# Order of the first recurrent mixer's output projection: one unit of the second half ahead of the first half's rest

## The reference

```
hmod = rms_norm(x, g_pre) * (1 + scale) + shift
y    = rms_norm(fn(hmod), g_post)
x    = x + weight * gate * y
```

```
hs = hs * rsqrt(mean(hs*hs) + EPS)                  # per head
hs = hs.reshape(B, S, 1024) * norm_w * sigmoid(o)
y  = hs @ ml_w_out                                  # 1024 x 1024
```

## Time and profile before

| | us |
|---|---|
| median of three runs | 1425.66 |
| lowest and highest run | 1424.58, 1426.38 |
| span of the profiled execution | 1421.9 |
| runs' median less that span | 3.8 |
| TensorE busy in the span | 1394.5 |
| VectorE busy | 1024.9 |
| ScalarE busy | 719.7 |
| mean granted clock, share of full | 0.998 |

### The profile page before, as it was taken

How to read it: one execution, slowest core, us unless ns; L and a number is a source line. 1 busy time by engine, 2 the same in 40 slices (tenths; PEclk the granted TensorE clock), 3 DMA queues, 4 the chain that set the end, 5 groups by cost and what they waited for, 6 DMA issues and landing times.

```text
span 1421.9 us, 18024 instructions
## 1 busy us (share of the span) xinstructions
PE 1394.5 (98%) x7310; PEld 1185.4 (83%) x7310; DVE 1024.9 (72%) x1296; ACT 719.7 (51%) x931; POOL 90.4 (6%) x118
## 2 busy tenths in 40 slices
PE   9999999998999999999999999999999999999997
PEld 8788888977888878888789978788888889998886
DVE  5887677987987668777767976678745654664865
ACT  5543356456444455343565676554334644555433
POOL 1000001001000010000000352100000100000000
PEclk9999999999999999999999999999999999999999
DMA  9898865855988848888535522478755454445542
GB/s 385 339 351 303 319 247 198 320 193 201 391 308 298 325 162 324 318 311 332 200 135 186 209 74 89 178 299 336 283 206 207 178 204 167 148 170 186 199 149 111
DMA packets 50498, 339.07 MB, mean 238 GB/s; under 512 B 6720, under 2 KB 8432, under 8 KB 10352
## 3 DMA queue, kind: packets, MB, share of 16 engines
q1 hardware_dynamic: 50416, 337.92, 63.8%
HBM read 336.81 MB, written 2.66 MB: 239 GB/s over the span
## 4 chain that ended last, share of the span: by engine, by line
PE 78%; DVE 12%; ACT 4%; DMA 2%; issue 2%; POOL 1%; SPq 0%; ACTq 0%; DVEq 0%; POOLq 0%
PE ps L1045 76%; DVE wlo L1704 4%; DMA raw<-units 2%; DVE hf L2126 2%; DVE M L1714 1%; ACT whi L558 1%; PE ps L1263 1%; PE ps L1154 1%; ACT hf L639 0%; POOL base L474 0%; POOL ssx L475 0%; DVE xboth L1779 0%; DVE wlo L1709 0%; PE ps L1528 0%; DVE xboth L2061 0%
## 5 line engine op out<-in xcount | busy, mean ns | idle before, releaser
L1045 PE MATMUL ps<-whi,xboth 128*128 128x512 f32 x2864 | 912.2, 393 | 6.5 <-DVE wlo L1709 1.7
L1045 PEld LDWEIGHTS ps<-whi,xboth 128*128 128x128 f32 x2864 | 538.3, 188 | 125.4 <-issue 4.7
L1704 DVE TENSOR_TENSOR wlo<-raw,whi 128x2048 fp32r<-128x2048 f32 x212 | 486.2, 2298 | 178.5 <-ACT whi L558 178.0
L1045 PE MATMUL ps<-wlo,xboth 128*128 128x512 f32 x1432 | 558.5, 390 | 0.0
L558 ACT ACTIVATE whi<-raw 128x2048 fp32r<-128x2048 f32 x218 | 416.9, 1915 | 170.8 <-DMA raw<-units 170.7
L1045 PEld LDWEIGHTS ps<-wlo,xboth 128*128 128x128 f32 x1432 | 269.5, 188 | 52.6
L1045 PE MATMUL ps<-xboth,whi 128*128 128x256 f32 (+1 forms) x1152 | 254.6, 310 | 0.1
L1045 PEld LDWEIGHTS ps<-xboth,whi 128*128 128x128 f32 x1152 | 187.9, 190 | 12.4 <-ACT hf L829 0.3
L1045 PE MATMUL ps<-xboth,wlo 128*128 128x256 f32 x704 | 198.1, 281 | 0.0
L1714 DVE SCALAR_TENSOR_TENSOR M<-M 128x1024 f32<-128x1024 f32 x160 | 189.3, 1220 | 0.1
L1045 PEld LDWEIGHTS ps<-xboth,wlo 128*128 128x128 f32 x704 | 133.9, 190 | 0.0
(11 more groups left out here) (242 smaller groups left out, 881.2 us busy)
## 6 DMA issues: line engine op xcount, KB each, us to landing
raw<-units SPq DMA_DIRECT2D x218, 1024.0 KB, 4.9
M<-ada_units SPq DMA_DIRECT2D x82, 1024.0 KB, 7.1
M<-units SPq DMA_DIRECT2D x10, 1024.0 KB, 5.3
gp<-gate_rows SPq DMA_DIRECT2D x7, 512.0 KB, 6.1
bias_copies<-bias_by_distance SPq DMA_DIRECT2D x1, 1536.0 KB, 9.6
M<-cvec SPq DMA_DIRECT2D x2, 512.0 KB, 4.4
x<-x_in SPq DMA_DIRECT2D x1, 1024.0 KB, 6.0
ada_a<-ada_units SPq DMA_DIRECT2D x1, 1024.0 KB, 20.0
```

The costliest lines, as they stand in the source:

```text
L1045: return pe.matmul(out, lhsT, rhs, start=start, stop=stop, skip_group_check=True)
L1704: dve.tensor_tensor(rest(u), landed(u), rounded(u).bitcast(F32), ALU.subtract).then_inc(w_lo, 1)
```

## The change

The loop over halves and units becomes a written list: (0,0), (1,0), (0,1), (0,2), (0,3), (1,1), (1,2), (1,3). `turn_am(1, (0, 1))`, the turns of the last head pair for both halves, stands between (0,0) and (1,0). The waits for `ml_lo`, the turn of the next stage's rows in the middle of (1,3), the `w_used` of half 1 and `y_done[0]` at the end of (0,3) are kept. No other engine's list is touched.

```diff
-                    for t in range(T):
-                        for u in range(4):
-                            if t == 0 and u == 2:
-                                turn_am(1, (1,))
-                            pe.wait_ge(S["ml_lo"], 2 * (u // 2) + t + 1)
-                            middle = None
-                            if (t, u) == (0, 1):
-                                middle = lambda: turn_am(1, (0,))
-                            if (t, u) == (1, 3):
-                                middle = lambda: turn_x(n + 1, 0)
-                            r = down(u0 + 12 + u, 2 * u, t, start=(u == 0), stop=(u == 3), middle=middle)
-                            if t:
-                                r.then_inc(w_used, 1)
-                        if t == 0:
+                    for t, u in ((0, 0), (1, 0), (0, 1), (0, 2), (0, 3), (1, 1), (1, 2), (1, 3)):
+                        if (t, u) == (1, 0):
+                            turn_am(1, (0, 1))
+                        pe.wait_ge(S["ml_lo"], 2 * (u // 2) + t + 1)
+                        r = down(u0 + 12 + u, 2 * u, t, start=(u == 0), stop=(u == 3),
+                                 middle=(lambda: turn_x(n + 1, 0)) if (t, u) == (1, 3) else None)
+                        if t:
+                            r.then_inc(w_used, 1)
+                        elif u == 3:
                             r.then_inc(y_done[0], 1)
```

## The result

The changed kernel takes 1429.29 us (median of 8 runs, 1427.93 to 1433.01), the kernel before 1425.53 us (8 runs beside it, 1423.03 to 1427.76). The ratio is 1.0025, 95% interval 1.0013 to 1.0036: slower by 3.6 us (1.9 to 5.1). The ratio is not the quotient of the two medians, so the two can differ by a few ten-thousandths. The forecast was 1428.9. The profiled execution took 1428.32 us with a span of 1426.5.

A forecast was written before the change was run, and what follows sets the result against it. TensorE, busy 98% of the span, was taken as the bound, so only its idle time counts. 0 us of work plus 3.27 us of waits on 1425.66 gave 1428.9 us; range 1426.6 to 1431.1.

The forecast's parts named there:

- The waits at the turns: First recurrent mixer's output projection: TensorE waits of 2.22 + 0.37 us for DVE's gating replace 1.61 us of waits.
- The first half's result: End of (0,3) in the projection: last product starts 3.56 us later, 2.72 of it from (1,0) moved ahead.
- The boundary: Boundary to the next feed-forward stage: DVE's fixed order passes on 3.27 us to TensorE's last release, at 341.87.
- what falls away on DVE: In the boundary, DVE's 0.29 us wait for ACT at 325.06 disappears, as ACT's work is only 2.0 us later.
- The wait at the turns of the rows: In the boundary, TensorE reaches the normed rows' turns before DVE's rows are ready and waits 1.0 us.
- The clock: Behind the turns, a possible fall to 1.2 GHz costing 1.7 us of lost work, left out of the sum.
- signs of being wrong: L1801 shifted but not TensorE's restart; granted clock under 1 between 306 and 312 us; first turns earlier than 305.
- the bound worked out from the earlier trace: From a clock fall behind a thin stretch at 820.0 in another stage: 1.7 us of lost work.
- The rival that I gave 0.17: The clock falls behind the new gap at the turns: +4.97 us in all, 1430.6 us; chance 0.17.
- the clock's case: The total if the clock falls behind the gap at the turns: +4.97 us, 1430.6 us; chance 0.17.
- Slower or the same: Whole kernel: 0.61 slower, 0.37 same, 0.02 faster, with about 0.2%, or 2.9 us, needed to tell a change.
- Queues: Load queue: unit 12's slot comes free at 309.4 instead of 316.7 us, the load lands earlier, worth nothing.

The follow-up runs named there:

- e3: Kernel before with only (1,0) moved ahead of (0,3), turns and their waits as before: 1427.18 us against 1425.06, ratio 1.0022.
- e5: Kernel before with only the turns of both halves moved between (0,0) and (0,1), old order of products: 1426.97 us against 1425.19, ratio 1.0016.
- r2: Changed kernel run again unchanged to see whether the clock falls: 1429.59 us (one run) against 1425.05 for the kernel before.
- r3: Changed kernel run again unchanged to see whether the clock falls: 1426.22 us (one run) against 1425.05 for the kernel before.
- r1: Changed kernel run again unchanged to see whether the clock falls: 1428.55 us against 1425.05 for the kernel before, ratio 1.0018.
- r4: Kernel before with DVE's last-pair gating ahead of unit 14's lower part and the first half's turns half a unit earlier, repeated: 1422.78 us against 1425.05, ratio 0.9984.
- e8: Changed kernel with DVE's last-pair gating ahead of unit 14's lower part and its last sums before its wait: 1425.64 us against 1425.19 (kernel before), ratio 1.0007.
- e1: Changed kernel with nine small products of ones between (0,0) and the turns, keeping TensorE busy: 1427.74 us against 1425.06 (kernel before), ratio 1.0021.

## Why the prediction was right

**The waits at the turns.** Predicted 2.22 + 0.37 us, with the turns at 305.39 and 306.17. Found at 305.39 and 306.17, less the offset.

**The first half's result.** Predicted 3.56 us late; 3.57, 3.58 and 3.52 in the profiles whose clock held. Apart: 2.72 for (1,0) (e3: 2.71) and 0.84 for the waits (e5: 0.82). The sum of the parts is the whole.

**The boundary.** Predicted to pass on 3.27; it passed on 3.16 to 3.21. The term that was a little off is what falls away on DVE, which I had as 0.29 us. From L1770 to the third of the lower parts (L1779, now L1774) DVE takes 4.97 us now and took 5.50, so 0.53 us of waiting for ACT fell away; POOL took some of it back (below). The wait at the turns of the rows was predicted at 1.0 us and is 0.98.

**The clock.** I left it out of the sum, because the gap of 2.22 us was nearer to the waits that had left the clock alone. It should have been a term with a chance of its own; two of four profiles say about a half, roughly. A granted clock under 1 between 306 and 312 us is among the prediction's own signs of being wrong, and the first profile shows it, at 0.72; r2 and r3 do not. The measured price, 1.6 us, is that of the bound worked out from the earlier trace rows, 1.7. The rival that I gave 0.17 was seen in two of four profiles of the changed kernel: in these four an execution is either about +3.2 or +4.8 at the last release. At even chances the mean is +4.0, an estimate from these figures. The Trainium skill ("TensorE: Matmul & The Clock Gate", Part 1) has idleness as what brings the half rate back; the trace agrees, and shows that one and the same gap does it in some executions only.

**What is luck in the number.** The forecast missed the median by 0.4 us. The interval of the measured loss is 1.9 to 5.1 us, so it holds the forecast's 3.3, the 4.0 with the clock in it and also the clock's case, 4.8. In r1 the two medians are 3.5 us apart, and the ratio gives 2.6. The mechanism is confirmed by the places in the profiles; the closeness of the total is partly luck.

**Slower or the same.** With 3.3 expected against 2.9 to be told, I gave 0.61 to slower by over 0.2%. The ratio is 0.25%, and r1 gave 0.18% with the interval 0.07 to 0.30: a loss is certain, its side of 0.2% is not.

**Queues.** That the earlier slot is worth nothing was not tried alone. ACT's wait for that load is gone and nothing behind it came earlier.

## What to carry to other kernels

A wait that is removed from the bound engine can be worth nothing if the removal delays what the next stage's serial chain starts from; ask which result leaves the stage first, and put no unit ahead of it. Here the cure for most of the waiting was on the engine that was waited for: its urgent operation belonged ahead of one that nobody needed yet. And a wait that is gathered in one place can cost more than the same waiting spread out: behind the gap of 2.2 us the clock fell in two of the changed kernel's four profiles.

## What the runs showed of the hardware

**The clock's fall is a matter of the single execution.** Beside the gap here, the second recurrent mixer has two places where the clock falls in some profiles, about 824 and 872 us. Two stretches of it in r4, then in e8:

```profile
820.00:840.00 20.00, 18.25 (x122) 15.10 (x122) 13.10 (x11) 16.02 (x33) 11.12 (x8) 1.00 0.15 53
860.00:880.00 20.00, 18.57 (x119) 16.25 (x119) 15.82 (x24) 13.79 (x31) 6.98 (x6) 1.00 0.03 5
```

```profile
820.00:840.00 20.00, 18.66 (x104) 15.15 (x102) 8.80 (x8) 13.55 (x29) 7.67 (x6) 0.83 0.15 53
860.00:880.00 20.00, 17.57 (x111) 15.92 (x111) 13.30 (x19) 13.99 (x37) 6.83 (x4) 0.83 0.08 35
```

The stage between the turns of the normed rows at its two ends takes 210.68 to 210.76 us in the four profiles without a fall there, 212.31 to 212.61 in the seven with one, 213.68 and 213.91 in two more, and 216.45 in e8, in which each of the two stretches has a mean of 0.83. No edit touches this stage. By the granted clock each fall costs 1.7 us of work, those in e8 twice that, as 0.83 over 20 us says; the stage is 1.6 to 1.9 us longer with one, 3.0 to 3.2 with two and 5.7 in e8. Why e8's last longer is not known. This is much of the spread of 2 to 8 us between runs of one kernel: of the 35 runs of the kernel before in the session of e1, the seven with a mean granted clock of 0.999 took 1421.8 to 1423.8 us, the three with 0.994 or 0.995 took 1428.8 to 1429.3. It is the reason why edits of 1 us had to be read in the profile, from a row near them, and not in the time. Up to 2.4 us more vary between TensorE's last release in the boundary and 717 us, with waits for the gated rows' lower part in some profiles; the cause of these is open.

**POOL and DVE.** Before, POOL's second copy in the boundary, and DVE's long subtraction beside it:

```profile
326.90 0.68 POOL L547 CAST xboth<-hf 128x256 fp32r<-128x256 f32 x1 [0.37 <-DVE hf L1790]
```

```profile
327.24 2.48 DVE L1704 TENSOR_TENSOR wlo<-raw,whi 128x2048 fp32r<-128x2048 f32 x1
```

and after, with DVE's rows beside it:

```profile
332.39 3.07 POOL L547 CAST xboth<-hf 128x256 fp32r<-128x256 f32 x1 [0.37 <-DVE hf L1785]
```

```profile
332.25 0.41 DVE L1774 TENSOR_TENSOR xboth<-hf,xboth 128x256 fp32r<-128x256 f32 x1
332.58 2.28 DVE L1699 TENSOR_TENSOR wlo<-raw,whi 128x2048 fp32r<-128x2048 f32 x1
...
335.49 0.42 DVE L1774 TENSOR_TENSOR xboth<-hf,xboth 128x256 fp32r<-128x256 f32 x1 [0.29 <-POOL xboth L547]
```

The same copy takes 0.68 us in one kernel and 3.07 in the other. It starts 0.34 us ahead of the subtraction (327.24) in the first, and the subtraction takes 2.48 us. It starts 0.19 us ahead (332.58) in the second, where the subtraction takes 2.28 and the copy ends 0.60 us after it (335.46), and DVE then waits 0.29 us for it. All profiles with a wait at the turns of the normed rows, and e8, have 3.06 or 3.07 us for this copy; the other five have 0.68 or 0.69. The Trainium skill, "SBUF — State Buffer", in "SBUF: two separate sides", says that a GpSimd operation that reads SBUF and a VectorE operation with two SBUF inputs exclude each other for a whole instruction, and that the one that starts first goes first. The subtraction has two such inputs. That the two exclude each other fits the rows; that the first goes first does not fit the recorded starts of the second case, and POOL's spans are rough. This was not tried by itself.
